# Cross attention's scores between query blocks, half of the keys behind the mix output, half of the values behind the last scores

## What is computed

```python
x = x + mix @ w_mix_out                                   # "mo" steps
x = x + cross_attention(rms_norm(x, norm_x), rms_norm(mem, norm_mem), w_xq, w_xkv, w_xo)
x = x + hierarchical_moe(rms_norm(x, norm_moe), ...)      # 32 experts, 192 MB of weights

def cross_attention(hn, mn, w_xq, w_xkv, w_xo):           # 4 heads of 256, 256 memory tokens
    q = (hn @ w_xq).reshape(b, l, X_HEADS, X_HEAD_DIM)    # "qx" steps
    kv = (mn @ w_xkv).reshape(b, m, 2, X_HEADS, X_HEAD_DIM)   # keys "kx", values "vx"
    k, v = kv[:, :, 0], kv[:, :, 1]
    s = jnp.einsum('blhd,bmhd->bhlm', q, k).astype(jnp.float32) * (X_HEAD_DIM ** -0.5)
    p = jax.nn.softmax(s, axis=-1).astype(v.dtype)
    o = jnp.einsum('bhlm,bmhd->blhd', p, v).reshape(b, l, D_MODEL)
    return o @ w_xo                                       # "xo" steps
```

## Time and profile before

| | |
|---|---|
| median of 3 runs | 968.09 us (967.49 to 968.67) |
| profiled execution | 967.55 us, its span 965.8 us |
| PE busy | 905.9 us (94%) |
| DVE, ACT, POOL busy | 445.0, 315.7, 139.1 us |
| bytes moved | 277.61 MB, mean 287 GB/s |
| granted TensorE clock, mean | 0.994 |

### The profile page before, as it was taken

The page is one execution under the profiler, slowest core; times in us unless marked ns, Lnnn a source line. Parts: engine busy times, 40 slices in busy tenths (PEclk is TensorE's granted clock), DMA queues, the critical chain, the costliest instruction groups (busy, mean ns, idle before and its releaser), DMA issues.

```text
span 965.8 us, 13766 instructions
## 1 busy us (share of the span) xinstructions
PE 905.9 (94%) x5671; PEld 624.6 (65%) x5671; DVE 445.0 (46%) x801; ACT 315.7 (33%) x515; POOL 139.1 (14%) x131
## 2 busy tenths in 40 slices
PE   5999999998999999999998999999999988998896
PEld 5899998887889999788774433434343433433432
DVE  4899977677977763464453111212121211210212
ACT  5555676667675334454340000000000000000112
POOL 1002369837850000000000000000000000000000
PEclk9999999999999999999999999999999999999999
DMA  8655553344355769656289899999999999999994
GB/s 225 185 178 172 175 160 110 126 132 131 111 162 152 227 207 359 224 190 246 60 329 362 355 422 421 421 421 421 421 420 421 421 422 420 421 421 421 420 421 184
DMA packets 108728, 277.61 MB, mean 287 GB/s; under 512 B 12850, under 2 KB 76514, under 8 KB 84090
## 3 DMA queue, kind: packets, MB, share of 16 engines
q1 hardware_dynamic: 108522, 276.21, 75.7%
q10 hardware_dynamic: 144, 0.52, 0.1%
HBM read 275.54 MB, written 1.05 MB: 286 GB/s over the span
## 4 chain that ended last, share of the span: by engine, by line
PE 62%; DMA 12%; DVE 7%; SPq 7%; ACT 5%; POOL 4%; issue 3%; ACTq 0%; DVEq 0%; POOLq 0%
PE bank L2007 14%; DMA moe<-in_w_e_up_dram 11%; PE bank L1577 9%; PE bank L1579 9%; PE bank L1578 9%; PE bank L2038 8%; SPq L417 7%; DVE lo_w L1005 2%; PE bank L2024 2%; PE bank L1974 2%; ACT hi_w L657 2%; POOL work L631 2%; PE bank L1763 1%; DVE work L1181 1%; PE bank L1882 1%
## 5 line engine op out<-in xcount | busy, mean ns | idle before, releaser
L2007 PE MATMUL bank<-moe,xg 128*64 128x512 f32 x1008 | 224.9, 595 | 15.3 <-DMA moe<-in_w_e_up_dram 9.9
L1005 DVE TENSOR_TENSOR lo_w<-raw_w,hi_w 128x2048 fp32r<-128x2048 f32 (+1 forms) x68 | 156.8, 2311 | 60.6 <-ACT hi_w L657 60.2
L1577 PE MATMUL bank<-u_hi,hi_w 128*128 128x256 f32 x616 | 177.0, 287 | 0.3 <-DVE work L1182 0.3
L1579 PE MATMUL bank<-u_hi,lo_w 128*128 128x256 f32 x616 | 174.0, 283 | 0.0
L2007 PEld LDWEIGHTS bank<-moe,xg 128*64 128x64 f32 x1008 | 73.7, 137 | 149.5 <-issue 148.8
L1578 PE MATMUL bank<-u_lo,hi_w 128*128 128x256 f32 x552 | 156.0, 283 | 0.0
L657 ACT ACTIVATE hi_w<-raw_w 128x2048 fp32r<-128x2048 f32 (+1 forms) x68 | 127.7, 1880 | 32.5 <-PE bank L1579 29.5
L1577 PEld LDWEIGHTS bank<-u_hi,hi_w 128*128 128x128 f32 x616 | 117.8, 191 | 3.8 <-issue 3.4
L2038 PE MATMUL bank<-moe,moe_buf 128*64 128x512 f32 x512 | 114.3, 596 | 5.9 <-DVE xg L1501 4.7
L1579 PEld LDWEIGHTS bank<-u_hi,lo_w 128*128 128x128 f32 x616 | 117.9, 191 | 0.0
L961 ACT ACTIVATE y_pair_hi<-bank 128x512 fp32r<-128x512 f32 x32 | 19.1, 598 | 291.3 <-PE bank L2038 291.3
(11 more groups left out here) (326 smaller groups left out, 1401.2 us busy)
## 6 DMA issues: line engine op xcount, KB each, us to landing
moe<-in_w_e_up_dram SPq DMA_DIRECT2D x64, 1024.0 KB, 26.0
moe<-in_w_e_down_dram SPq DMA_DIRECT2D x64, 1024.0 KB, 26.4
moe<-in_w_e_gate_dram SPq DMA_DIRECT2D x62, 1024.0 KB, 26.0
raw_w<-in_w_in_dram SPq DMA_DIRECT2D x34, 1024.0 KB, 5.5
raw_w<-in_w_ssm_out_dram SPq DMA_DIRECT2D x8, 1024.0 KB, 5.5
raw_w<-in_w_xkv_dram SPq DMA_DIRECT2D x8, 1024.0 KB, 6.3
raw_w<-in_w_att_out_dram SPq DMA_DIRECT2D x4, 1024.0 KB, 5.1
raw_w<-in_w_mix_out_dram SPq DMA_DIRECT2D x4, 1024.0 KB, 8.8
```

Source lines behind the costliest of these rows:

```text
L1005: tt(lo_w[:, m % RING, 0:w], raw_w[:, m % RING, 0:w], hi_w[:, m % HI_RING, 0:w].bitcast(F32), ALU.subtract).then_inc(lo_done, 1)
L1577: mm(dst, left[0], right[0], start=first, stop=False)
L1579: return mm(dst, left[1], right[0], start=False, stop=last)
L2007: last = mm(ps[64 * a:64 * a + 64, :], xg[:, k, P * o + CAP * a:P * o + CAP * a + CAP], w[:, k % (KT // 2), :], start=(k == 0), stop=(k == ...
```

## The change

The order of the steps and the places of five loads change; the products are the same. On PE the order becomes so0..7, kx0..3, mo, kx4..6, the transposes of `xn1`, kx7, vx c = 0, qx0..2, scores of head 0, qx3, qx4, scores 1, turned 0, qx5, qx6, scores 2, turned 1, values 0, qx7, values 1, turned 2, scores 3, vx c = 1, turned 3, values 2, the first half of xo c = 0, values 3, the second half.

The two halves of a head's scores share one bank (4 or 5), with one semaphore and one maximum for both. The units are loaded in the new order. `m_lo` (the low part of the normalised mem) moves from `work` to `xdt`, `qxT` from `u` to `gates`; so the loads of (1, 0) and (2, 1) move behind the last values and scores, and (9, 1) comes before (5, 1).

```diff
@@ where things lie @@
-        m_lo = place("m_lo", [P, KT, SEQ], "work", F32R, skip=6 * KB)
+        m_lo = place("m_lo", [P, KT, SEQ], "xdt", F32R)
-        qxT = place("qxT", [P, KT, SEQ], "u")
+        qxT = place("qxT", [P, KT, SEQ], "gates", skip=8 * KB)
@@ steps (the units follow the same order) @@
-                 + [f"kx{b}" for b in range(8)] + [f"mo{c}{i}" for c in range(2) for i in range(NT)]
-                 + [f"vx{c}{i}" for c in range(2) for i in range(NT)] + [f"qx{b}" for b in range(8)]
+                 + [f"kx{b}" for b in range(4)] + [f"mo{c}{i}" for c in range(2) for i in range(NT)]
+                 + [f"kx{b}" for b in range(4, 8)] + ["vx00", "vx01"] + [f"qx{b}" for b in range(8)] + ["vx10", "vx11"]
@@ SP @@
-                if name == "mo00":
+                if n == UN["so7"] + RING:
                     first_load(0, 0)
                     first_load(0, 1)
                     sp.wait_ge(tr_ready, 8)
-                    first_load(1, 0)
                     first_load(1, 1)
                 if name == "vx00":
                     sp.wait_ge(mix_ready, 8)
                     first_load(2, 0)
-                    first_load(2, 1)
...
+            wait_used(sp, UN["vx11"])
+            first_load(1, 0)
+            first_load(9, 1)
             over_ring(5, 1, raw_slot=3)
-            sp.wait_ge(xs_ready, NT * X_HEADS)
-            first_load(9, 1)
+            sp.wait_ge(xs_ready, X_HEADS)
+            first_load(2, 1)
             over_ring(7, 0, raw_slot=4)
@@ ACT @@
-            for b in range(8):
+            for b in range(4):
                 evac(f"kx{b}", kxT[:, b, :])
             split_hi_through(UN["mo00"] + 2)
             norm_stats_by_tile("mo", 2, xn1)
+            for b in range(4, 7):
+                evac(f"kx{b}", kxT[:, b, :])
+            transposed_hi(a_hi)
+            evac("kx7", kxT[:, 7, :])
             mem_values(0)
-            transposed_hi(a_hi)
-            mem_values(1)
-            for b in range(8):
-                evac(f"qx{b}", qxT[:, b, :], scale=(D // X_HEADS) ** -0.5)
...
+            for b in range(8):
+                evac(f"qx{b}", qxT[:, b, :], scale=(D // X_HEADS) ** -0.5)
+                if b in (2, 4, 6):
+                    cross_exps(b // 2 - 1)
+            cross_hi(0)
+            cross_exps(3)
+            cross_hi(1)
+            mem_values(1)
+            cross_hi(2)
+            cross_hi(3)
             split_hi_through(UN["xo00"] + 2)
@@ DVE @@
-            for j in range(4):
-                split_lo_through(UN[f"kx{j}"] + 2)
+            split_lo_through(UN["mo00"] + 1)
             dve.wait_ge(x_in, 32)
             residual_and_norm("mo", 2, xn1)
-            split_lo_through(UN["vx10"])
+            split_lo_through(UN["vx01"])
             columns_of(0, g_x, a_hi, a_lo, NT)
-            split_lo_through(UN["qx0"])
-            for j in range(4):
-                split_lo_through(UN[f"qx{j}"] + 2)
+            split_lo_through(UN["qx2"])
...
             cross_max(0)
+            cross_probs(0)
+            split_lo_through(UN["qx3"])
+            cross_max(1)
+            cross_probs(1)
+            split_lo_through(UN["vx10"])
+            cross_turned(0)
+            cross_max(2)
+            cross_probs(2)
+            split_lo_through(UN["vx11"])
+            cross_turned(1)
+            cross_max(3)
+            cross_lo(0)
+            cross_probs(3)
+            cross_lo(1)
+            cross_turned(2)
+            split_lo_through(UN["xo00"])
+            cross_turned(3)
+            cross_lo(2)
+            split_lo_through(UN["xo01"])
+            cross_lo(3)
             split_lo_through(UN["xo00"] + 2)
@@ PE @@
+            for b in range(4):
+                cross_keys(b)
             for c in range(2):
                 tm_steps("mo", c, a_parts, mix_lo, (4, 8))
+            for b in range(4, 7):
+                cross_keys(b)
+            transposes(xn1)
+            cross_keys(7)
             tm_steps("vx", 0, m_parts)
...
             def x_scores(h):
+                wait_evac(pe, f"qx{2 * h + 1}")
+                if h < 2:
+                    pe.wait_ge(seg_ready, 32)
+                else:
+                    pe.wait_ge(xexp_done, NT * (h - 1))
...
+            cross_queries(0)
+            cross_queries(1)
+            cross_queries(2)
             x_scores(0)
+            cross_queries(3)
+            cross_queries(4)
             x_scores(1)
+            x_turned(0)
+            cross_queries(5)
+            cross_queries(6)
+            x_scores(2)
+            x_turned(1)
+            x_values(0)
+            cross_queries(7)
+            x_values(1)
+            x_turned(2)
+            x_scores(3)
+            tm_steps("vx", 1, m_parts)
+            x_turned(3)
+            wait_evac(pe, "vx11")
+            x_values(2)
...
-            tm_steps("xo", 0, a_parts, xo_lo, (2, 4))
+            tm_steps("xo", 0, a_parts, xo_lo, (2, 4), between=lambda: x_values(3))
```

## The result

The changed kernel takes 970.91 us (median of 13 runs, 968.3 to 972.77), the kernel before beside it 967.19 us (13 runs, 965.5 to 969.08). The ratio is 1.0036, with a 95% interval of 1.0027 to 1.0045: slower by 3.7 us. The forecast was 971.3 us.

A forecast was written before the change was run, and what follows sets the result against it. DMA bounds the experts' second part, but PE sets when its full queue starts. Stalls of 11.0 us against 7.65 gave 3.4, by times 3.0, taken as 3.2; 967.55 + 3.2 = 970.75, median 0.54 above: 971.3 us, range 966.0 to 973.6.

The forecast's parts named there:

- The key stall: Behind the mix output, kx6 waits for ACT's copy of kx4 behind the norm's roots: 4.6 us, about 4.4 shown idle.
- The transposes: Behind kx6, they wait for DVE's columns behind unit 57's low part: 1.3 us instead of 0.4.
- the clock: Half clock at kx6 and the transposes behind the key stall: nothing in the sum, 0 to 1.7 us kept for the range.
- Scores between the queries: Scores placed behind queries show no idle time on PE; the queries hide the softmax of heads 0 and 1.
- Values 1: Behind qx7, values 1 wait 0.95 us for DVE's `cross_turned(1)`, which stands behind a `lo_w` split.
- Values 2, xo: Stalls of 0.4 us ahead of values 2, 1.5 ahead of xo's second half, 0.45 at xo's first sum.
- The sum: PE's stalls from the keys to xo: 11.0 us after, 7.65 before; 3.4, or 3.0 by times, taken as 3.2.
- The end follows: What PE gains or loses ahead of its first expert product moves the end by the same amount.
- The loads: The four moved loads, out at about 468.7 us, fit into idle DMA time and cost nothing.
- A: Rival, chance 0.18: at kx6 nothing replaces the removed stalls, the copy of kx4 doesn't hold it; faster, 965.8 us.
- B: Rival, chance 0.18: DMA hides the experts' later start, or the key stall is half; no change, 968.1, up to 970.
- C: Rival, chance 0.12: unhidden half clock at the key stall and again at values 1, 1.7 us more: 973.0 us.

The follow-up runs named there:

- keys_only: Kernel before with only kx4 to kx7 moved behind the mix output; 5.6 us slower than the kernel before.
- filled_wait: Changed kernel with 34 unused key-like matmuls on PE where kx6 waits; first copy of qxT at 65.30 us instead of 66.23.
- combined_values: Changed kernel with vx c = 0 directly behind mo, head 3's values ahead of xo, `cross_turned(1)` ahead of a `lo_w` split; 962.12 us beside 967.18.
- late_router: Kernel before with four unused float32 products 128x512 on PE ahead of the router's logits; 3.4 us longer.
- loads_only: Kernel before with only the moved loads and the two moved tiles, no PE step moved; ratio 1.0005.
- scores_only: Kernel before with scores between the queries and head 3's values between xo's halves, keys and values' second half in their old places; 3.7 us slower.
- copies_columns: Changed kernel with ACT's kx4 and kx5 copies ahead of the roots and DVE's columns ahead of unit 57's low part; xo's first sum 4.9 us earlier.
- values3_first: Changed kernel with head 3's values ahead of xo's first half; +2.3 us against the kernel before instead of +3.7.
- copies_first: Changed kernel with ACT's copies of kx4 and kx5 ahead of the norm's square roots; 5.1 us slower than the kernel before.

## Why the prediction was right

**The key stall.** Forecast 4.4 us of idle time ahead of kx6, released by ACT's copy behind the root. Measured 4.33, in the changed kernel and in keys_only. Right in place, cause and size.

**The transposes.** Forecast 1.3 us of wait instead of 0.4, and nothing for the clock. At full clock the place comes out: filled_wait shows 1.00 idle there, and its kx7 starts 48.37 us behind the first copy of kxT, where 408.0 - 359.5 = 48.5 was forecast. In the changed kernel the clock fell, kx6 took 1.57 us longer, and the wait shrank to 0.42: 0.9 us more than forecast in all, within the 0 to 1.7 kept for it. The end of qx0, where its copy starts, was forecast at 421.8 + 2.88 = 424.7, so 65.2 us behind the first copy of kxT; filled_wait shows 65.30, the changed kernel 66.23. So the clock was the mis-sized term: put at nothing in the sum, it measured 0.9 us. The Trainium skill, in TensorE: Matmul & The Clock Gate (What's actually happening), takes the throttled state for the default, which activity releases; this case agrees, with 0.54 behind 4 us without a matmul, and 1.00 once they were filled. The same section of the Trainium skill says that the point at which the clock changes varies, there for a kernel's first matmuls. This case fits that in its middle: two kernels with the same 4.33 us of idle time show 0.91 and 0.81 over the 18 us around it, one execution each.

**Scores between the queries.** Forecast without waits, and so they are: no row of scores has idle time ahead. Values 1 were forecast to wait 0.95 us and wait 0.37 (0.20 shown). This is a mis-sized term: DVE's split ahead of `cross_turned(1)` began 25.1 us behind the first copy of qxT (451.08 - 425.94), and I had it at 26.0 (453.0 - 2.29 - 424.7). One maximum for both halves lets a head's second exponential follow 0.46 or 0.47 us behind the first; before, with a second maximum between, it was 0.86. So 0.4 us of the 0.9 is what the single maximum shortens, which I hadn't priced; for the rest of it no run here gives a cause. The place was right, since combined_values, with the copy ahead of the split, shows no wait there.

**Values 2, xo.** Forecast 0.4 ahead of values 2, 1.5 ahead of xo's second half and 0.45 behind it; measured 0.42 (0.25 shown), 1.58 (1.41 shown), and 0.2 (1.04 instead of 0.83).

**The sum.** Forecast +3.2 at xo's first sum, measured +3.2 (123.96 less 120.76). The place and the cause of the stalls are right, but that the sum is met to 0.1 us is luck, since errors cancel: +0.9 of clock, against -0.6 and -0.25 for the two terms that came out smaller. So is part of the close hit in absolute time: the median of before, on which the 971.3 us stands, was 968.09 over three executions and is 967.19 over thirteen, and against the thirteen the change cost 3.7 us, not 3.2. The end follows (late_router). The loads cost nothing (loads_only).

**Where the gain went.** The change does remove what it was to remove: by the rows, 4.6 us of waits of scores and softmax and 0.7 of `lo_w`, for which the waits at values 1, values 2 and xo bring 2.6 (0.37 + 0.42 + 1.58 + 0.2). The queries' start moved by 66.23 + 10.9 (the values that went behind it) - 72.00 = 5.1 us later, and from there to xo's sum 1.9 us came back. scores_only shows what the late values are worth in this: without them the last head's softmax has no cover (2.43 us, and 1.7 more of clock), and the scores between the queries are themselves a loss.

**The rivals.** A (no wait in place of those removed): not in the changed kernel, yet its condition is the right one, as copies_columns shows: -1.6 where it forecast -2.3; two short waits are left. B (hidden): its hiding is refuted by late_router, its key stall of half the size by the 4.33 us. C (clock): its first half was there, at the key stall, with 0.9 instead of 1.7; not at values 1, where the clock is 1.00.

**What stays open.** The medians of several kernels stand higher than xo's sum says: the changed kernel by 0.5 us, loads_only by 0.9, values3_first, scores_only and filled_wait by 1.0 to 1.2, copies_first by 1.2. For copies_first the runs point at the clock: the mean granted clock of its five executions is 0.986 to 0.992, that of the twenty of the kernel before beside it 0.989 to 0.997. Which part of it is clock, and where in the kernel it is lost, isn't shown, since only one execution of each kernel was traced.

## What to carry to other kernels

Before a step is moved into a gap, list what its bank needs on the engine that empties it: ACT works in order, and a copy that stands behind two waits is as late as they are. When such a wait is cured, look at once for the one behind it on another engine, because curing one alone may gain nothing (copies_first). Work that goes into such a gap must need nothing from the chain that just ended, and must last in its own banks until the copies come (here the 10.9 us of a value step, where 5.8 us of keys didn't suffice); and the late half of such a step goes where the last softmax has no cover.

## What I had not expected of the hardware

A long wait of PE cost twice. Waits of 4.33 us (in three kernels) and 4.40 us, and one of 2.43 with 0.56 close behind, were each followed by matmuls at about half clock (0.50 to 0.60 granted, 0.41 us instead of 0.28 for 128x256). That cost 0.9 us where another wait hid part of it and 1.7 us where none did. Waits of 1.4 us, such as those of the softmax before, were followed by none.

Between the two the outcome is open. All fourteen traced executions have a wait of 2.7 us near 900 us. In before it is the one of the earlier trace rows, with 0.52 behind it, and in keys_only, copies_columns and loads_only the granted clock falls there too. In the other ten it stays at 1.00, as in the changed kernel:

```profile
901.76 0.39 PE L2003 MATMUL bank<-S,xn_hi 128*128 128x256 f32 x1 [2.71 <-DVE S L1424]
```

```profile
902.00:904.00 2.00, 2.00 (x18) 1.97 (x18) 0.71 (x2) 0.00 (x0) 0.00 (x0) 1.00 1.00 418
```

So the earlier trace rows shows what can follow such a wait, and not what must.

The router's stretch has the same trait without any long wait. From xo's first sum to the experts' first product the work is the same in all kernels but late_router, and yet it took 30.93 to 30.99 us in the six executions where the granted clock from 494 to 516 us was 1.00, 31.38 to 31.48 in the four with 0.92, and 33.03 to 33.16 in the three with 0.84. The six are not free of it: in each of them the clock falls a little later, between 522 and 536 us, behind a wait of 1.55 us among the experts' first products, as here in combined_values:

```profile
522.00:524.00 2.00, 1.14 (x6) 0.88 (x8) 0.69 (x1) 0.00 (x0) 0.00 (x0) 0.86 1.02 430
524.00:526.00 2.00, 2.00 (x6) 0.53 (x4) 0.00 (x0) 0.00 (x0) 0.00 (x0) 0.50 0.93 389
526.00:528.00 2.00, 2.00 (x10) 0.73 (x8) 0.00 (x0) 0.00 (x0) 0.00 (x0) 0.78 0.06 16
```

The other eight have the same wait of 1.55 us and keep 1.00 there. The time from the experts' first product to the end goes with these falls: 452.70 to 453.09 us in the five executions with none behind the router (the last 15 us apart, where the clock falls in all fourteen), 454.07 to 454.51 in the five with one between 522 and 536 us alone, 453.86 to 454.15 in the three with the one near 900 alone, and 454.65 in copies_columns, which has both. That a fall costs this 1 to 2 us is read from the grouping; no run tests it.

This fits the two spans of before and of the changed kernel, which differ by only 2.1 us (965.8 and 967.9) where the medians differ by 3.7: the traced execution of before has the fall near 900 us and takes 454.15 us from the experts' first product on, that of the changed kernel has none and takes 452.85. The mean granted clock varies in untraced executions as well, from 0.989 to 0.997 among those of the kernel before. So a single profile can be off by up to 2 us at the experts' start and by 1 to 2 us behind it, and only column xo and medians over several runs resolve an edit of this size.
